# One program for attention and expert lookup: loops replaced by a planned straight order, tiles worked in smaller groups, the sample rows last

## The reference

```python
q_a, k_a, v_a, q_b, k_b, v_b = project(xp, pos_p, attn_norm[l], w_in[l])      # 1024 -> 2304 columns
o_a, _ = banded_attention(q_a, k_a, v_a, sink_l)
o_b = combine_dilations([dilated_branch_prompt(q_b, k_b, v_b, d) for _, d in DILATIONS])
xp = mix_out(xp, o_a, o_b, out_norm_a[l], out_norm_b[l], w_out[l])
xp = xp + peer_ffn(rms_norm(xp, ffn_norm[l]).reshape(-1, D_MODEL), peer_w_q[l], peer_sub_keys[l], peer_u[l], peer_v[l])

def peer_ffn ... block(hc):
    q = (hc @ w_q).reshape(PEER_CHUNK, PEER_HEADS, 2, PEER_QDIM // 2)
    sc = jnp.einsum('chpd,hpkd->chpk', q, sub_keys)
    s1, i1 = lax.top_k(sc[:, :, 0], PEER_TOPK); s2, i2 = lax.top_k(sc[:, :, 1], PEER_TOPK)
    ... top 16 of the 16 x 16 sums -> eid (16 experts for each of 8 heads), gate = softmax
    act = jax.nn.gelu(jnp.einsum('cd,chkd->chk', hc, u[eid]))
    return jnp.einsum('chk,chkd->cd', gate * act, v[eid])
```

## Time and profile before

| | |
|---|---|
| three runs | 3911.89, 3938.85 (median), 3945.16 us |
| span of the profiled execution | 3919.0 us |
| PE, DVE, POOL, ACT busy | 80%, 60%, 60%, 18% |
| moved by DMA | 1224.76 MB |

### The profile page before, as it was taken

The page is one execution under the profiler, slowest core; times in us unless marked ns, Lnnn a source line. Parts: engine busy times, 40 slices in busy tenths (PEclk is TensorE's granted clock), DMA queues, the critical chain, the costliest instruction groups (busy, mean ns, idle before and its releaser), DMA issues.

```text
span 3919.0 us, 42716 instructions
## 1 busy us (share of the span) xinstructions
PE 3134.2 (80%) x9160; PEld 1539.4 (39%) x9160; DVE 2346.3 (60%) x6264; ACT 707.5 (18%) x2060; POOL 2356.5 (60%) x2204
## 2 busy tenths in 40 slices
PE   6997648787888888888888888878887777877777
PEld 3544434333444444443444343434433333333332
DVE  1221386666666666666666666666666577666665
ACT  0111111111222212221222122211222111111111
POOL 0000036777677757775777577766777577657772
PEclk9998769999999999999999999999999999999999
DMA  6541349999899989998999899989999999989995
GB/s 232 182 169 61 148 139 339 354 354 345 317 351 344 358 315 358 344 359 313 340 358 366 325 346 346 354 330 340 349 339 338 347 385 365 363 300 349 352 353 173
DMA packets 356567, 1224.76 MB, mean 313 GB/s; under 512 B 40176, under 2 KB 64904, under 8 KB 354800
## 3 DMA queue, kind: packets, MB, share of 16 engines
q0 software_dynamic: 297216, 1082.26, 75.7%
q1 hardware_dynamic: 59160, 140.36, 10.1%
HBM read 1208.16 MB, written 49.00 MB: 321 GB/s over the span
## 4 chain that ended last, share of the span: by engine, by line
DMA 33%; PE 29%; issue 15%; DVE 9%; POOL 8%; DVEq 4%; ACT 1%; SPq 1%; POOLq 1%; ACTq 0%
DMA ring<-in_peer_v,win_v 17%; PE acc L822 14%; DMA ring<-in_peer_u,win_u 11%; POOL ring L548 8%; DMA wo_sb<-in_w_out 3%; PE pS L769 3%; PE pT L624 3%; PE pM L796 3%; DVE ring L1394 2%; PE pA L624 2%; DVEq L1325 1%; DMA ring<-in_x_all 1%; DVE topv L1326 1%; PE pM L750 1%; DVEq L1344 1%
## 5 line engine op out<-in xcount | busy, mean ns | idle before, releaser
L822 PE MATMUL acc<-ring,diag 128*128 128x512 f32 x4096 | 1999.8, 617 | 520.5 <-DMA ring<-in_peer_v,win_v 460.4
L1394 DVE CUSTOM_DVE_ANT_0 ring<-ring,hpair 128x1024 f32<-128x1024 f32 x1024 | 1248.0, 1221 | 828.8 <-DMA ring<-in_peer_u,win_u 825.6
L548 POOL DMA_INDIRECT ring<-in_peer_v,win_v x1024 | 1177.3, 1150 | 563.5 <-issue 247.0
L548 POOL DMA_INDIRECT ring<-in_peer_u,win_u x1024 | 1121.4, 1095 | 429.4 <-issue 281.0
L822 PEld LDWEIGHTS acc<-ring,diag 128*128 128x128 f32 x4096 | 730.8, 193 | 1555.1 <-issue 1190.5
L1050 ACT ACTIVATE diag<-idn,wv 128x128 f32<-128x128 f32 x1024 | 378.8, 395 | 670.6 <-PE acc L822 548.6
L796 PE MATMUL pM<-wbuf,TT 128*128 128x256 f32 (+1 forms) x1152 | 263.3, 382 | 0.0
L796 PEld LDWEIGHTS pM<-wbuf,TT 128*128 128x128 f32 x1152 | 221.9, 193 | 59.2 <-issue 31.3
L769 PE MATMUL pS<-wo_sb,PT 128*128 128x512 f32 x288 | 160.6, 687 | 90.5 <-DVE PT L1126 50.9
L545 POOL COPY VB<-ring 128x512 f32 x8 | 4.9, 613 | 311.7 <-ACT ring L930 311.7
L624 PE MATMUL pT<-wbuf,TT 128*128 128x512 f32 x288 | 125.1, 592 | 0.0
(11 more groups left out here) (210 smaller groups left out, 2449.1 us busy)
## 6 DMA issues: line engine op xcount, KB each, us to landing
wo_sb<-in_w_out SPq DMA_DIRECT2D x72, 512.0 KB, 6.3
out_dil_s<-in_cache_dil SPq DMA_DIRECT2D x8, 4092.0 KB
ring<-in_peer_u,win_u POOLq DMA_INDIRECT x1024, 6.2
ring<-in_peer_v,win_v POOLq DMA_INDIRECT x1024, 6.2
wbuf<-in_w_in SPq DMA_DIRECT2D x4, 2048.0 KB, 16.8
wbuf<-in_w_q SPq DMA_DIRECT2D x1, 8192.0 KB, 22.6
ring<-in_x_all SPq DMA_DIRECT2D x9, 512.0 KB, 4.0
x<-in_x_all SPq DMA_DIRECT2D x9, 512.0 KB, 6.3
```

Of the source, the lines that this page charges most:

```text
L548: pool.indirect_dma_start(buf, None, table, bass.IndirectOffsetOnAxis(win, 0)).then_inc(landed, 16)
L822: m = pe.matmul(acc[:, half * 512:(half + 1) * 512], diag[:, j % 4, :], v_ring[j % RING][:, half * 512:(half + 1) * 512], start=False, sto ...
L1394: dve.tensor_tensor_reduce(u_ring[j % RING], u_ring[j % RING], h_cur, 1.0, 0.0, ALU.mult, ALU.add, dots[:, par, j:j + 1]).then_inc(u_used, 1)
```

## The change

The program is rewritten. What it computes is the same; what moves and what is issued is not:

- **No loops.** A planner in Python puts *stages* (a projection chunk, one step of a head's attention, a query, a ranking) and places into one list `PLAN`, and each engine issues its part of that list as straight code. A stage carries the PE and DVE time that the planner books for it and how many places must lie between it and the stage before it.
- **The gathers begin after tile 0.** Projection, attention and output of tile 0 come first, then the rest is put between the places. Counted in the built order, the last of this other work stands at place 666 of 1058, and the 391 places after it hold only gathers, dots and weighings.
- **Groups.** Tiles are projected in the groups 0, 1, 2-3, 4-5, 6-7 with the sample, and go through output and queries in the groups 0, 1, 2-3, 4-5, 6, 7 with the sample. `w_in` is loaded 5 times (9.44 MB each), `w_out` (4.19 MB) and `w_q` (8.39 MB) 6 times, through two buffers of 2 MB (`W_LOADS`).
- **x and h** are written to scratch and read back (`x2_scr`, `h_scr`); x also comes transposed, so that PE transposes no x.
- **v rows on two engines.** Of 1032 weighings PE does 830 and DVE 202, as a multiply-add of 128x1024 into `accs` (L1875). In places 0 to 666 the split is 456 and 193.
- Attention runs over the t+1 key blocks that tile t has, for each tile. POOL has nothing but gathers and waits. v is gathered 18 places behind u (`LAG`); both rings still have four buffers.

The core of the diff:

```diff
-                head = 2 * p + par
...
-                pool.tensor_copy(win_v[:, par, :], win_u[:, par, :]).then_inc(win_cp, 1)
...
-                    col = 0 if isinstance(p, int) and p == 3 and par == 1 else (head + 1) * TOPK
-                    pool.tensor_copy(win_u[:, 1 - par, :], idx_all[:, ds(col, TOPK)]).then_inc(win_set, 1)
-                    hold(pool, "pool", win_set, nxt + 1)
-                hold(pool, "pool", win_cp, s + 1)
-                for j in range(TOPK):
-                    if not last:
-                        hold(pool, "pool", u_used, TOPK * nxt + j - RING + 1)
-                        fetch(u_ring[j % RING], peer_u, win_u[:, 1 - par, j:j + 1], u_in[j % RING])
-                    hold(pool, "pool", v_used, TOPK * s + j - RING + 1)
-                    fetch(v_ring[j % RING], peer_v, win_v[:, par, j:j + 1], v_in[j % RING])
...
+IN_GROUPS = ((0,), (1,), (2, 3), (4, 5), (6, 7, SAMPLE))
+GROUPS = ((0,), (1,), (2, 3), (4, 5), (6,), (7, SAMPLE))
+ORDER = tuple(t for g in GROUPS for t in g)
+RU, RV = 4, 4
+LAG = 18
...
+    def ranks(h):
+        out = []
+        for s, tiles in bands_of(group):
+            for t in tiles:
+                out += [("r0", g, h, 0, 0.0, 3.3, t), ("r1", g, h, 0, 0.0, 2.2, t)]
+            out += [("r2", g, h, 0, 0.0, 1.9, tiles), ("r3", g, h, 0, 0.0, 2.0, tiles)]
+        return out + [("ge", g, h, 0, 0.0, 0.0), ("gd", g, h, 1, 0.0, 0.9)]
...
+PHASES = (
+    (projection_stages(0) + attention_stages(0) + output_stages(0),),
+    (ranking_stages(0), projection_stages(1) + attention_stages(1)),
+    (output_stages(1),),
+    (ranking_stages(1), projection_stages(2) + attention_stages(2) + attention_stages(3)),
+    (output_stages(2),),
...
+    def offer(self, p):
+        for i in sorted((i for i, q in enumerate(self.queues) if q), key=self.left, reverse=True):
+            s = self.queues[i][0]
+            if s[3] > self.rested[i] or self.pe + s[4] > self.dma + 12.0 or self.dve + s[5] > self.dma + 9.0:
+                continue
+            if self.due(p) or (self.pe + self.dve + s[4] + s[5]) / 2 <= self.dma + 3.0:
+                self.take(i)
+                self.spent += s[4] + s[5]
+                return True
+        return False
...
+            self.dve += 1.35 if u is not None else 0.0
...
+            if v is not None:
+                self.on_pe[p] = v[0] == "s" or self.pe + 1.95 <= self.dve + 1.45
...
+W_LOADS = (
+    [IN_0[0], IN_0[2], IN_0[4], OUT[0][1], *QUERY[0], OUT[1][1], *QUERY[1], OUT[2][1], *QUERY[2],
+     OUT[3][1], *QUERY[3], OUT[4][1], *QUERY[4], OUT[5][1], QUERY[5][0], QUERY[5][2]],
+    [IN_0[1], IN_0[3], OUT[0][0], *[("in", 1, c) for c in CHUNKS], OUT[1][0],
+     *[("in", 2, c) for c in CHUNKS], OUT[2][0], *[("in", 3, c) for c in CHUNKS], OUT[3][0],
+     *[("in", 4, c) for c in CHUNKS], OUT[4][0], OUT[5][0], QUERY[5][1], QUERY[5][3]],
+)
+W_AT = {x: (b, i) for b in range(2) for i, x in enumerate(W_LOADS[b])}
...
+            for p in range(PLACES):
...
+                    elif u[0] == "f" and u[1] % TOPK == 0:
+                        pool.wait_ge(r_idx, RANKED[u[1] // P, u[1] % P // TOPK])
+                    fetch_u(U_ENTRY[p], peer_u, rows_at(u))
...
+                if v is not None:
+                    fetch_v(V_ENTRY[p], rows_at(v))
...
+                need(pe, k_ev, n)
+                for k in range(KD):
+                    m = pe.matmul(pA[:, 0:width_of(GROUPS[g])], wchunk[b][:, k, (i % 4) * P:(i % 4 + 1) * P],
+                                  hT[g][:, k, :], start=(k == 0), stop=(k == KD - 1))
...
+            def weigh(p):
...
+                dve.wait_ge(ac_in[i % 2], 16 * (i // 2 + 1))
+                dve.wait_ge(v_in[e % RV], 16 * (e // RV + 1))
+                D_()
+                dve.scalar_tensor_tensor(accs[:, i % 2, :], v_ring[:, e % RV, :], wv[:, section % 2, j:j + 1],
+                                         accs[:, i % 2, :], ALU.mult, ALU.add).then_inc(v_dve, 1)
```

More of the change, by code:

```diff
@@ new lines @@
+OUT = [[("out", g, half) for half in range(2)] for g in range(len(GROUPS))]
+QUERY = [[("q", g, quarter) for quarter in range(4)] for g in range(len(GROUPS))]
+W_LOADS = (
[4 more added lines that the diff above has]
+     *[("in", 4, c) for c in CHUNKS], OUT[4][0], OUT[5][0], QUERY[5][1], QUERY[5][3]],
+)
@@ L657, in _ @@
[L657 to L670 removed]
+            seen = {"ze": 0, "zv": 0, "ox": 0, "hv": 0, "ng": 0, "ke": 0, "sm": 0, "pe": 0}
@@ L827, in acc_start @@
-            def acc_start(t, rows=P):
-                pe.wait_ge(mx_h, after(mx_h, t + 1))
-                if not (isinstance(t, int) and t == 0):
-                    pe.wait_ge(fin_free, after(fin_free, t))
-                for half in range(2):
-                    m = pe.matmul(acc[0:rows, half * 512:(half + 1) * 512], idn[:, 0:rows],
-                                  x2[:, half * 512:(half + 1) * 512], start=True, stop=False,
-                                  skip_group_check=True)
-                m.then_inc(acc_init, 1)
@@ L1111, in rsqrt @@
                 y = nw_i[r, c].bitcast(F32)
-                for _ in range(3):
+                for step in range(3):
                     D_()
```

2611 lines of the change are left out of this document (1505 added, 1106 removed).

## The result

The changed kernel takes 3949.0 us (median of 20 runs, 3924.1 to 3962.5), the kernel before 3919.9 us (20 runs; the 3938.85 shown ahead was the median of the first three). The ratio is 1.0052, interval 1.0036 to 1.0068: 0.5% slower, within the 1% that counts as no change. The forecast was 3845 us. The profiled run has a span of 3953.3 us, and it splits at the points of the prediction. The gathers' lines give the points (duration ns min/median/max, first and last start us); place 667 starts at 2877.

The account below looks back on a forecast made before the run. DMA was taken to bound the middle at 2369 us, with PE and DVE close; 149 + 2580 + 1077 + 18 gave 3824 us of span, about 3845 us measured. Its own range was 3770 to 3900, for 8 in 10 3690 to 4030.

Parts of the forecast that it names:

- the points of the prediction: Span split at first gather, place 666 and last gather: 149, 2580, 1077 and 18 us, together 3824 us.
- The start: Until the first gather, only tile 0 stands before it on the path: 149 us, bounds 135 and 200.
- Bytes: Whole kernel moves 1305 MB, 6.5% more than before; 867 MB of them in the middle, places 0 to 666.
- The engines' sums in the middle: Places 0 to 666: DMA 2369 us, PE about 2000, DVE 2110 plus drains, POOL up to 2230; none over DMA's.
- POOL's allowance of 600 us: Places 0 to 666: each of 860 dots and DVE weighings costs a gather 0.7 us, added to POOL's 1632 us.
- I take 336 GB/s, nearer to the dense stretches since the spacing between steps is kept: Places 0 to 666: 867 MB at this rate take 2580 us, 3.87 us a place, bounds 2456 and 2797.
- rival D: Last stage, places 667 on: TensorE's clock falls to 1.2 GHz, 220 us more, 4065 us; chance 0.05.
- The last stage: Places 667 to 1057: 2.88 us for each of 374 pairs of gathers, 1077 us, bounds 1036 and 1111.
- C: Rival: gain lost to about nothing by half-strength ring emptying, a 200 us prologue or slower end; 3900 to 3978 us; chance 0.18.
- B: Rival: in the middle the u and v rings empty behind PE or DVE and POOL stops; time 4060 us; chance 0.19.
- the 2675 us: Middle, places 0 to 666: threshold above which rival B decides, 4.0 us a place or 324 GB/s.
- signs that I named for B: Middle: DMA share under 0.86, POOL waiting long for `u_used` or `v_pe`, PE waiting for ACT, DVE or `wbuf` pieces.

Follow-up runs that it names:

- e11: Changed kernel with half the columns of each of the 1024 dots on DVE left out; 0.9966 of the kernel before.
- e6: Changed kernel with more places ahead of five kinds of steps, so that their loads have landed; 0.9755 of the kernel before.
- e8: Changed kernel with half the columns of each PE weighing but a tile's first left out; 0.9942 of the kernel before.
- e2: Changed kernel with the planner's pacing rule called and steps taken only when due, last one at place 964; 0.9820 of the kernel before.
- e7: Changed kernel with steps taken only when due and the five longer rests (places left ahead of a step); 0.9632 of the kernel before.
- e5: The changed kernel itself, unaltered, run again on the chip of e6 to e8; 1.0063 of the kernel before.

## Why the prediction was wrong, step by step

- **The start.** The forecast of 149 us for the first gather was right: 158.8, within the bounds of 135 to 200.
- **Bytes.** They were right too: 1307.2 MB for 1305. In the middle 316 GB/s over 2718 us are 859 MB, for 867.
- **The engines' sums in the middle.** PE took 1972 us for about 2000, DVE 1923 for 2110, POOL 1479 + 306 = 1785 for up to 2230. None was too low. In DVE's sum one term doesn't follow from its factors: 55 index steps of six operations of 0.43 us are 142 us and not 240, which brings the sum near the measured 1923. POOL's allowance of 600 us for gathers held by DVE was too high: its 1316 gathers were busy for 1479 us, 242 more than 1316 x 0.94. A gather that starts in a DVE weighing does wait, as the timeline shows (1.92 us, forecast 1.7), but shorter dots hardly changed the time (e11). The Trainium skill, SBUF — State Buffer, section Who interferes with whom, infers that descriptor generation needs only the write interface, which two-input instructions leave free. The trace disagrees as far as the issue of an indirect gather goes, which lasted 1.92 us here instead of 0.94; which part of it is held isn't shown.

```profile
1552.17 1.28 DVE L1875 SCALAR_TENSOR_TENSOR accs<-v_ring,wv,accs 128x1024 f32<-128x1024 f32 x1
1552.34 1.92 POOL L975 DMA_INDIRECT u_ring<-in_peer_u,idx  x1 [3.93 <-DVE dots L1835]
```

- **The step that failed: "I take 336 GB/s, nearer to the dense stretches since the spacing between steps is kept".** It was 316 GB/s, 2718 us for 2580. I had taken the spacing of steps as enough for loads too, and priced the waits for pieces in the middle at nothing. The order holds loads that pass through DRAM or through one buffer: weight pieces three places apart, q, x of a second tile, the sample's rows. There were 237 us of direct waits for them, and 933 us in which POOL had no free slot. e6 shows that moving their users away gives back 180 us of the middle with the same bytes, out of the long stops. e8 and e11 show that the slack of DVE and PE, which I had named as the reason for not taking more than 336, is not it: with half the columns of the weighings or of the dots the middle is only some 40 us shorter. The spacing itself was also too dense: e2, with no longer rest, has a middle 234 us shorter, of which the tail gives 215 back. How the 138 us divide between the two isn't shown.
- **The clock.** I had watched it in the last stage alone. There it was 0.94 (rival D is out). In the middle it was 0.85, where the earlier trace rows have 0.99 with PE at 0.84 busy. PE's share alone doesn't explain it: in the middle PE was busy for 0.73 of the time at 0.85, and in the last stage for 0.72 at 0.94. What differs is how PE stood idle: in the middle 50 pieces of over 5 us, 397 us of its 747 us of idle time, and one in the last stage. A weighing pass took 679 ns on average over the whole for 617:

```profile
L1220 PE MATMUL acc<-v_ring,diag 128*128 128x512 f32 x3288 | 1785.3, 679 | 798.8 <-ACT diag L1462 443.4
```


  That PE's sum came near was partly luck: it was priced at the higher clock, and the lower one was made up for by a count of work that was too high. What the lower clock costs the whole was not isolated; e8 only says that 243 us less of PE in the middle, at a clock that is lower still, are worth 1.2%.
- **The last stage.** It took 1060 us for 1077. The full DMA moved 377 GB/s at a share of 0.99, more than the 366 that I had worked out from a stretch with other work in it. The Trainium skill, DMA: Bandwidth & Descriptors, section Specifications, gives about 358 GB/s per core, as half of a stack's 716 GB/s for two cores. The trace goes above it for 1060 us. This program ran on one core, and so the prediction was wrong to take the figure as a limit for it.
- **The rivals.** C is what happened, B's mechanism at half its strength: the middle was over the 2675 us from which I said that the gain is lost. Most signs that I named for B were there: POOL waiting for `u_used` and `v_pe`, PE waiting for ACT, and PE waiting for pieces of `w_in`. The share was 0.87, just short of the sign (under 0.86). But B put it down to steps that follow each other too closely on PE, ACT and DVE. Of the long stops 21 of 29 hold a wait for a load; the short ones, 590 us, may well be what B describes. I gave C 0.18 and should have given the waits for loads a term.
- **What the order says.** The planner has a rule that would spread the other work, and nothing calls it. The last step at place 666 was in my prediction, but not that the room behind it was left unused by omission. e2 prices it at 2.4%, its split of the weighings included.
- **Small things.** The forecast time had 20 us added to the span, from the difference between a median of three runs and a span. Over 20 runs the kernel before has a median 1 us above its profiled span, so this term was an accident of three runs, and it hid 20 of the 129 us of error. Of the slices, DMA was 0.44 busy in the first 500 us and not half, and several of the later ones stand at 8 tenths; nothing in the sum hangs on either.

These questions stay open: which share of e6's gain is each load's, as the single rests of pieces and x gave nothing clear of noise and q's was not run alone; how much would be won by issuing the store ahead of the weight pieces (e7's trace says that it lands sooner with none ahead, but nothing here reorders SP's queue); what the clock itself costs.

## What to carry to other kernels

Where engines run in order and feed shallow rings, add up for every step the time from the moment its load *can* be issued (buffer free, earlier store landed, pieces ahead of it in the queue) to its landing, and compare it with the places in between. Here a wait for 512 KB stopped DVE and POOL for about 20 us and PE for 13, and no busy share shows such a wait before it happens. Judge the removal of such waits by several together: two of them removed singly gave nothing that could be measured, five together gave 3.1%, and the same 88 MB were worth more once they were gone. And read from the built order where the work has gone, not from the rule that is meant to place it.

## What the runs showed of the hardware

- A store of 512 KB issued 0.5 us behind two loads of 2 MB landed after 16.8 us (16.4 to 18.6 in e7). With no such load ahead of it, it landed after 5.1 and 6.7 us with gathers in flight (e7), and after 2.9 us with nothing in flight.
- One core's DMA moved 377 GB/s for 1060 us, with gathers of 4 KB rows almost alone.
- The granted clock was 0.99 with PE 0.84 busy before. With PE at 0.71 to 0.73 it was 0.85 in the middle of the changed kernel, where PE had 50 idle pieces of over 5 us, and 0.94 (e5: 0.97) in the last stage, which had one (e5: none). With half the columns (e8) it was 0.76 at 0.65 and 0.61 at 0.64.
- Where DMA was full, the last stage took 1051 us at a granted clock of 0.61 with half the columns of the weighings (e8), and 1047 us at 0.97 with all of them (e5).
- The issue of a gather that started 0.17 us into a 1.28 us DVE instruction with two SBUF inputs took 1.92 us, ending 0.8 us after it; undisturbed it takes 0.94.
